# Second expert stage: four experts at a time with 32 places each, instead of two with 64

## The reference, cut to what matters

```
def hier_moe(v, ...):                       # 256 tokens
    grp_prob = softmax(vt @ w_grp + b_grp); p_grp, g_sel = top_k(grp_prob, 1)      # one of 4 groups
    p_in, e_sel = top_k(softmax(expert logits in the group), 2)                    # two of its 8 experts
    combine[t, e] = p_grp * p_in / sum(p_in)                                       # weights, 32 columns
    for e in range(32):
        hdn = silu(vt @ w_gate[e]) * (vt @ w_up[e])        # 1024 -> 512
        y = y + (combine[:, e:e+1] * hdn) @ w_down[e]      # 512 -> 1024
return rms_norm(h + y, g_final)
```

## Time and profile before

| | us |
|---|---|
| median of three runs (range) | 2190.81 (2186.52 to 2191.62) |
| the profiled execution | 2189.51 |
| its span, first to last instruction | 2187.8 |
| of that, second expert stage (from its first product at 1707.87) | 479.9 |
| TensorE busy / DMA mean rate over the span | 95% / 323 GB/s |

### The profile page before, as it was taken

How to read it: one execution, slowest core, us unless ns; L and a number is a source line. 1 busy time by engine, 2 the same in 40 slices (tenths; PEclk the granted TensorE clock), 3 DMA queues, 4 the chain that set the end, 5 groups by cost and what they waited for, 6 DMA issues and landing times. The chain is left out here.

```text
span 2187.8 us, 25313 instructions
## 1 busy us (share of the span) xinstructions
PE 2083.4 (95%) x10244; PEld 1024.6 (47%) x10244; DVE 538.5 (25%) x1147; ACT 366.7 (17%) x628; POOL 98.6 (5%) x185
## 2 busy tenths in 40 slices
PE   6989999989999999999999999899899999999998
PEld 4677676643333333333333333364464444444443
DVE  2356453432121122112111212222343100000001
ACT  2133421210000000000000000213341111111112
POOL 2010052000000000000000000100030000000000
PEclk9999999999999999999999999999999999999999
DMA  9332245559999999999999999834253699999995
GB/s 340 107 126 103 76 182 206 214 234 428 427 428 429 428 429 429 428 429 428 428 429 427 429 429 427 317 116 167 66 207 135 257 426 429 428 428 430 428 428 227
DMA packets 98558, 707.05 MB, mean 323 GB/s; under 512 B 12314, under 2 KB 17932, under 8 KB 61516
## 3 DMA queue, kind: packets, MB, share of 16 engines
q1 hardware_dynamic: 98508, 706.36, 78.6%
HBM read 705.29 MB, written 1.05 MB: 323 GB/s over the span
## 5 line engine op out<-in xcount | busy, mean ns | idle before, releaser
L1647 PE MATMUL ps<-ring,arena 128*64 128x512 f32 x2048 | 449.8, 593 | 24.6 <-DMA ring<-in_moe_w_gu 24.6
L1647 PEld LDWEIGHTS ps<-ring,arena 128*64 128x64 f32 x2048 | 145.6, 137 | 323.3 <-issue 266.5
L2821 PE MATMUL ps<-ring,arena 128*64 128x512 f32 x1024 | 225.4, 593 | 8.5 <-DMA ring<-in_w_up 6.7
L1674 PE MATMUL ps<-ring,arena 128*64 128x512 f32 x1024 | 225.1, 592 | 0.0
L2821 PEld LDWEIGHTS ps<-ring,arena 128*64 128x64 f32 x1024 | 78.8, 137 | 151.8 <-issue 151.8
L1698 ACT ACTIVATE arena<-arena 128x512 f32<-128x512 f32 x32 | 20.1, 630 | 769.8 <-DVE arena L1729 769.8
L1041 PEld LDWEIGHTS ps<-arena 128*128 128x128 f32 x1088 | 128.6, 196 | 41.9 <-issue 38.9
L1674 PEld LDWEIGHTS ps<-ring,arena 128*64 128x64 f32 x1024 | 73.2, 137 | 146.5 <-issue 128.1
L1041 PE MATMUL ps<-arena 128*128 128x128 f32 x1088 | 138.1, 284 | 2.6 <-DVE arena L1033 2.6
L2074 PE MATMUL ps<-ring 128*128 128x512 f32 (+1 forms) x320 | 139.7, 586 | 0.7 <-ACT ring L2453 0.6
L2842 PE MATMUL ps<-ring,arena 128*64 128x512 f32 x512 | 113.4, 595 | 0.0
(11 more groups left out here) (571 smaller groups left out, 1934.5 us busy)
## 6 DMA issues: line engine op xcount, KB each, us to landing
ring<-in_moe_w_gu SPq DMA_DIRECT2D x128, 2048.0 KB, 23.9
ring<-in_moe_w_down SPq DMA_DIRECT2D x64, 2048.0 KB, 21.3
ring<-in_w_down SPq DMA_DIRECT2D x32, 2048.0 KB, 13.3
ring<-in_w_gate SPq DMA_DIRECT2D x32, 2048.0 KB, 14.9
ring<-in_w_up SPq DMA_DIRECT2D x32, 2048.0 KB, 17.2
ring<-in_w_in SPq DMA_DIRECT2D x22, 2048.0 KB, 8.4
ring<-in_ada_w SPq DMA_DIRECT2D x12, 2048.0 KB, 9.6
ring<-in_w_out SPq DMA_DIRECT2D x6, 2048.0 KB, 8.7
```

Of the source, the lines that this page charges most:

```text
L1647: last = M.matmul(ps[halves[j], 4 + which, :], xgT[buf][:, k, CAP * ee:CAP * ee + CAP], w[:, k2, at:at + 512], start=False, stop=(k == KD ...
L1674: last = M.matmul(ps[halves[j], 6, :], yT[:, k % KH, halves[k // KH]], w[:, k % KH, 512 * j:512 * j + 512], start=False, stop=(k == 2 * KH ...
L2821: last = M.matmul(ps[halves[j], 4 + which, :], xgT[:, k, halves[j]], w[j][:, k, :], start=(k == 0), stop=(k == KD - 1))
```

## The change

An expert of the second stage gets CAP2 = 32 places in a pass instead of 64, and four experts (QUAD) are handled at a time, 8 quads instead of 16 pairs. With 29 tokens in the fullest expert there is still one pass.

- The output partitions are split into four strips of 32 (quads). Gate and up products are made for two experts at a time: pair (0, 1), then pair (2, 3), each 8 slices x 2 experts. The down products take all four experts side by side: 2 x 4 x 4 = 32 matmuls of 128 x 32 x 512, after all four down slots have arrived.
- Gather, transposes and scatter come once for a quad instead of once for a pair, with the shapes they had.
- A quad has 12 loads in a ring of 6 slots: gate 0 to 3 in slots 0 to 3, up 0 and 1 in slots 4 and 5, up 2 and 3 in slots 0 and 1, down 0 to 3 in slots 2 to 5. s_done rises once for each pair's gate, once for each pair's up, and by 2 at the end of the down products, which gives back four slots at once. ExpertLoads gets the count of loads and of rounds as parameters; the first experts use it with their old numbers.
- VectorE makes the one-hot of four experts by one comparison of 128 x 256 elements with broadcast operands, and the gated one by one multiplication, instead of 4 + 4 small operations for a pair. A row of numbers 0 to 255 (iota_all) is made once by GpSimd early in the second mixer.
- The tables of places and gates have 36 columns for this stage; GpSimd's later_tables is gone there, two small copies on VectorE and four more steps in pass_count come in.

```diff
-    loads2 = ExpertLoads("experts2", gate_up_down2, 2)
+    loads2 = ExpertLoads("experts2", gate_up_down2, 3 * QUAD, 2, MAXP2)
+    quads = [slice(CAP2 * e, CAP2 * (e + 1)) for e in range(QUAD)]
+    def quad_onehot(onehot, slots, first, ready):
+        V.tensor_tensor(onehot.rearrange("p t (e c) -> p t e c", e=QUAD), rep(rep(first, QUAD), T), bcast(slots, CAP2),
+                        ALU.is_equal).then_inc(ready, 1)
...
             def load(item, base):
-                for s, (src, k, w) in enumerate(self.chunks(item)):
-                    sp.wait_ge(self.s_done, base * self.steps + s // self.per_done + 1)
-                    sp.dma_start(slot(s, k, w), src).then_inc(self.full[s], 16)
+                for c, (src, k, w) in enumerate(self.chunks(item)):
+                    sp.wait_ge(self.s_done, base * self.steps + (c + self.count - SLOTS) // self.per_done + 1)
+                    sp.dma_start(slot(c % SLOTS, k, w), src).then_inc(self.full[c % SLOTS], 16)
...
                         for which in range(2):
-                            w = [loads.arrived(pe, 2 * which + j, i) for j in range(2)]
-                            for k in range(KD):
-                                for j in range(2):
-                                    last = M.matmul(ps[halves[j], 4 + which, :], xgT[:, k, halves[j]], w[j][:, k, :],
-                                                    start=(k == 0), stop=(k == KD - 1))
-                            last.then_inc(s_done, 1)
+                            for pair in ((0, 1), (2, 3)):
+                                w = {e: loads.arrived(pe, QUAD * which + e, i) for e in pair}
+                                for k in range(KD):
+                                    for e in pair:
+                                        last = M.matmul(ps[quads[e], 4 + which, :], xgT[:, k, quads[e]], w[e][:, k, :],
+                                                        start=(k == 0), stop=(k == KD - 1))
+                                last.then_inc(s_done, 1)
...
-                        w = [loads.arrived(pe, 4 + j, i, 4, 1024) for j in range(2)]
+                        w = [loads.arrived(pe, 2 * QUAD + e, i, 4, 1024) for e in range(QUAD)]
                         pe.wait_ge(s_yTt, i + 1)
                         for d in range(2):
                             for k in range(KH):
-                                for j in range(2):
-                                    last = M.matmul(ps[halves[j], (4, 7)[d], :], yT[:, k, halves[j]],
-                                                    w[j][:, k, 512 * d:512 * (d + 1)], start=(k == 0), stop=(k == KH - 1))
+                                for e in range(QUAD):
+                                    last = M.matmul(ps[quads[e], (4, 7)[d], :], yT[:, k, quads[e]],
+                                                    w[e][:, k, 512 * d:512 * (d + 1)], start=(k == 0), stop=(k == KH - 1))
                             if d == 0:
                                 last.then_inc(s_dh, 1)
-                        last.then_inc(s_done, 1)
+                        last.then_inc(s_done, 2)
```

More of the change, by code:

```diff
@@ L21 @@
 CAP = 64
+CAP2 = 32
+QUAD = 4
 class Chain:
@@ L880, in program @@
     iota_row = sb("iota_row", [P, 2, CAP])
+    MAXP2 = T * P // CAP2
+    NI2 = NE + QUAD
+    slot_of2, gate_of2 = ar(13600, T, NI2), ar(13600 + T * NI2, T, NI2)
+    iota_all = masks[:, 0:T, :].rearrange("p a b -> p (a b)")
     passes = sb("passes", [1, 1], I32)
@@ L913, in first_slots, with pass_count @@
         dve.wait_ge(s_slot, 1)
-        vv(V.tensor_scalar(slot_of[:, :, 0:NE], tmp2, -1.0, None, ALU.add))
-    def pass_count(rank_bank):
+        vv(V.tensor_scalar(table[:, :, 0:NE], tmp2, -1.0, None, ALU.add))
+    def pass_count(rank_bank, cap):
         vv(V.tensor_reduce(cmax[:, 0:1], ps[:, rank_bank, 64:96], X_AXIS, ALU.max))
-        vv(V.tensor_scalar(cmax[:, 1:2], cmax[:, 0:1], float(CAP), 1.0, ALU.is_gt, ALU.add))
-        for b in range(2, MAXP):
-            vv(V.scalar_tensor_tensor(cmax[:, 1:2], cmax[:, 0:1], float(b * CAP), cmax[:, 1:2], ALU.is_gt, ALU.add))
+        vv(V.tensor_scalar(cmax[:, 1:2], cmax[:, 0:1], float(cap), 1.0, ALU.is_gt, ALU.add))
+        for b in range(2, T * P // cap):
+            vv(V.scalar_tensor_tensor(cmax[:, 1:2], cmax[:, 0:1], float(b * cap), cmax[:, 1:2], ALU.is_gt, ALU.add))
         vv(V.tensor_copy(passes[0:1, 0:1], cmax[0:1, 1:2]))
@@ L964, in program, with __init__ @@
     class ExpertLoads:
-        def __init__(self, name, chunks, per_done):
-            self.name, self.chunks, self.per_done = name, chunks, per_done
-            self.steps = SLOTS // per_done
+        def __init__(self, name, chunks, count, per_done, most):
+            self.name, self.chunks, self.count, self.per_done, self.most = name, chunks, count, per_done, most
+            self.steps = count // per_done
+            self.rounds = count // SLOTS
             self.full = [sem(f"{name}_slot{s}_full") for s in range(SLOTS)]
@@ L983, in load_rest @@
         def load_rest(self, sp, items):
-            n = sp.value_load(passes[0:1, 0:1], min_val=1, max_val=MAXP)
+            n = sp.value_load(passes[0:1, 0:1], min_val=1, max_val=self.most)
+            for c, (src, k, w) in enumerate(self.chunks(0)):
+                if c >= SLOTS:
+                    sp.wait_ge(self.s_done, (c - SLOTS) // self.per_done + 1)
+                    sp.dma_start(slot(c % SLOTS, k, w), src).then_inc(self.full[c % SLOTS], 16)
             def load(item, base):
-                for s, (src, k, w) in enumerate(self.chunks(item)):
-                    sp.wait_ge(self.s_done, base * self.steps + s // self.per_done + 1)
-                    sp.dma_start(slot(s, k, w), src).then_inc(self.full[s], 16)
+                for c, (src, k, w) in enumerate(self.chunks(item)):
+                    sp.wait_ge(self.s_done, base * self.steps + (c + self.count - SLOTS) // self.per_done + 1)
+                    sp.dma_start(slot(c % SLOTS, k, w), src).then_inc(self.full[c % SLOTS], 16)
             with sp.Fori(0, items - 1) as q:
@@ L999, in load_rest, with arrived @@
             return n
-        def arrived(self, pe, s, i, k=KD, w=512):
-            pe.wait_ge(self.full[s], i * 16 + 16)
-            return slot(s, k, w)
+        def arrived(self, pe, c, i, k=KD, w=512):
+            pe.wait_ge(self.full[c % SLOTS], i * (16 * self.rounds) + 16 * (c // SLOTS + 1))
+            return slot(c % SLOTS, k, w)
     halves = [slice(CAP * j, CAP * (j + 1)) for j in range(2)]
@@ L1555, in _ @@
             V.tensor_tensor(gate_of[:, :, 0:NE], gate_of[:, :, 0:NE], bcast(gs, NE), ALU.mult).then_inc(s_gat1, 1)
-            pass_count(4)
+            pass_count(4, CAP)
             V.memset(y21, 0.0).then_inc(s_y21, 1)
@@ L1976, in program @@
     s_k11 = sem("ranks2_ready")
-    s_gat2 = sem("gates2_normalised")
+    s_iota2 = sem("places_numbered")
     s_slot2 = sem("first_slots2_ready")
@@ L1985, in gate_up_down2 @@
     def gate_up_down2(q):
[L1987 to L1990, removed]
-    loads2 = ExpertLoads("experts2", gate_up_down2, 2)
+        quad = [QUAD * q + e for e in range(QUAD)]
+        return ([(one(w_gt, e).rearrange("(p k) n -> p k n", k=KD), KD, 512) for e in quad]
+                + [(one(w_up, e).rearrange("(p k) n -> p k n", k=KD), KD, 512) for e in quad]
+                + [(one(w_d2, e).rearrange("(p k) n -> p k n", k=4), 4, 1024) for e in quad])
+    loads2 = ExpertLoads("experts2", gate_up_down2, 3 * QUAD, 2, MAXP2)
[3 more added lines that the diff above has]
+                        ALU.is_equal).then_inc(ready, 1)
     FIRST = 6
@@ L2758, in _ @@
             dve.wait_ge(s_e12, 2)
-            vv(V.tensor_tensor(gate_of[:, :, 0:NE], gate_of[:, :, 0:NE], sel, ALU.mult))
-            vv(V.tensor_reduce(gs, gate_of[:, :, 0:NE], X_AXIS, ALU.add))
+            vv(V.tensor_tensor(gate_of2[:, :, 0:NE], gate_of2[:, :, 0:NE], sel, ALU.mult))
+            vv(V.tensor_reduce(gs, gate_of2[:, :, 0:NE], X_AXIS, ALU.add))
             vv(V.tensor_tensor(gs, gs, gsum, ALU.mult))
             vv(V.reciprocal(gs, gs))
-            V.tensor_tensor(gate_of[:, :, 0:NE], gate_of[:, :, 0:NE], bcast(gs, NE), ALU.mult).then_inc(s_gat2, 1)
-            pass_count(4)
+            vv(V.tensor_tensor(gate_of2[:, :, 0:NE], gate_of2[:, :, 0:NE], bcast(gs, NE), ALU.mult))
+            vv(V.tensor_copy(gate_of2[:, :, NE:NI2], gate_of2[:, :, 0:QUAD]))
+            vv(V.tensor_scalar(slot_of2[:, :, NE:NI2], slot_of2[:, :, 0:QUAD], -float(CAP2), None, ALU.add))
+            pass_count(4, CAP2)
             V.memset(y22, 0.0).then_inc(s_y22, 2)
@@ L2771, in program, with expert_quads @@
     s_p13 = sem("final_weight_loaded")
-    def expert_pairs(loads, x_tok):
+    def expert_quads(loads, x_tok):
         KH = 4
-        NP = NE // 2
+        NQ = NE // QUAD
         xgT, sg, y, yT = ar(7168, KD, P), ar(8192, 512), ar(8704, KH, P), ar(9216, KH, P)
@@ L2794, in _ @@
```

(30 more changed lines are left out.)

25 lines of the change are left out of this document (13 added, 12 removed).

## The result

The changed kernel takes 2196.85 us, median of 6 runs (2195.74 to 2199.59); the kernel before, beside it, 2186.73 (2185.03 to 2191.62). The ratio is 1.0036, 95% interval 1.0026 to 1.0047: slower, by about 8 us by the ratio (the two medians are 10.1 apart). The time lies inside the range that was given, the sign is the wrong one.

A forecast was written before the change was run, and what follows sets the result against it. The prediction took the DMA load stream as the bound, by a hair over TensorE. Terms -5.2 - 2.0 - 0.4 = -7.6, + 1.1 + 2.5 = -4.0 us gave 2185.5 us (2186.8 beside the median), 8-in-10 range 2181 to 2201.

The forecast's parts named there:

- The bound: Second expert stage: DMA sets the pace by a hair, 29.3 us a pair, of which TensorE needs 28.8.
- TensorE's work, four strips at once: Down products of four experts run side by side, 7.0 us; some 14 us a quad saved, all beside the stream.
- rival 5: Strips not side by side, +46 us, or more than 32 tokens in an expert, +470 us; chance 0.02.
- The end: Last quad: all other products done before its last down load lands, so the 5.3 us wait shrinks; gain 5.2 us.
- The hole at the start: Stream gap at 1736 to 1740 goes because slots come free sooner; gain 2.0 us.
- Routing: One comparison replaces four small ones on the path to the first gather; 0.4 us saved.
- Four slots at once: Next loads wait for the down products' end, 2.5 us of stream left; 0.15 us x 7 quads, 1.1 us lost.
- far end: Upper bound for the four-slot wait: 2.4 us in each of 7 quads, 16.8 us.
- The clock: TensorE idles 4.0 us ahead of down products; one down in four cold at full price, 2.5 us lost.
- Rival 2: Queue runs dry behind the down products, 2.4 us in each of 7 quads: +9.2, with clock +12, 2200 to 2203; chance 0.17.
- Rival 4: Every down starts cold, 7 x 1.7 us, start-up hidden or nearly: +5.4, 2196; chance 0.08.
- Rivals 1 and 3: 1: start-up and clock cost nothing, 2183, chance 0.23; 3: stream's own holes and charges eat the gain, 2190, chance 0.08.

The follow-up runs named there:

- filler ahead of the down products: Changed kernel plus four extra 128 x 128 x 512 matmuls before the wait for the down loads; 2193.31 us, ratio 1.0017 to the kernel before.
- the filled kernel with 4.0 left: Changed kernel with extra matmuls in every wait of the second expert stage and 3/4 of the down products; 2184.56 us, ratio 0.9978 to the kernel before.
- the filled kernel with 2.2 left: Changed kernel with extra matmuls in every wait of the second expert stage, all down products kept; 2198.40 us, ratio 1.0036 to the kernel before.

## Why the prediction was wrong, point by point

*The bound.* Right: the stream of loads sets the pace, what TensorE saves inside it is worth nothing, the gains lie at its ends and holes.

*TensorE's work, four strips at once.* Right, and with it rival 5 is out: 64 records in 7.07 us where 7.0 was worked out from L267.

*The end.* Right: -5.0 against -5.2. *The hole at the start.* Gone as said, -2.9 against -2.0. *Routing.* Of the stage's 1.2 us earlier start at most 0.2 can be from it: TensorE's wait in the routing ahead of the comparison already ended 1.0 us earlier in this execution.

*Four slots at once: the step that failed.* The prediction named the wait, the 2.5 us left (2.2 to 2.3 measured) and both ends, and chose 0.15 us a quad, on the argument that a start-up of 2.6 us runs beside the last 2.5 us of stream, since "2.5 us is nearer to filled than 1736.75 was". It isn't: at full clock and 2.2 us left the price is 1.8 us on average, at 3.1 still 0.9, and it takes 4.0 to hide it. The term was put at 1.1 us; 15.4 was measured. That alone turns -4 into +10. The rest brings it to the +7.2 between the profiles: clock -0.8 (1.7 for 2.5), hole -0.9, start -0.8, smaller items -0.8, end +0.2.

The trace before held the very case. The prediction took the queue at 1736.75 to be "almost empty" and the median of 12.2 us in the earlier trace rows to be 2.3 us over an empty queue's. By the landing times the up load ahead was there at 1738.92 and the first down load at 1746.70: 2.2 us of stream were left, as in the changed kernel, and 7.78 - 4.89 = 2.9 us were lost. The hole that the change removes and the dips that it brings in are one thing, once before and seven times after. The 2.4 us kept as far end, 16.8 in all, came out near the 15.4, though by a sum that isn't the one of the trace. Of the two loads behind the "empty queue" of the earlier trace rows one was issued with 0.7 us left, and it landed after 7.47 us, where the other took 7.57: there too what was left hid next to nothing.

*The clock.* Sized at 2.5 us for seven down products; one in four of the bound of 1.7 us would be 0.43 and not 0.36 a quad, so 3.0, and the sum -3.5 and not -4.0. Right in kind: the waits ahead of the down products were 3.1 to 4.8 us where 4.0 was worked out, and in five of eight quads of this profile the down products were cold in part, clock 0.71 to 0.83. What it costs: filler ahead of the down products bought about 4 us (ratio 1.0017 against 1.0036 and 1.0040), of which 1.7 is the last quad's down products, which the prediction left out, because nothing is queued behind it. The dips hid the rest: once a start-up is paid, down products that end 1.7 us later cost only a few tenths more.

*The rivals.* Rival 2 was the case, with its mechanism and nearly its price (+9 to +12 us given, +8 by the ratio measured; as times 2200 to 2203 and 2196.85); it had 0.17. What it held against itself, that the DMA engines "were already idle" at 1736.75, was not so. Rival 4's 2196 is the nearest number, by coincidence: not every down product starts cold, start-ups aren't hidden, and with every down product at full clock six quads still lost 1.8 us each. Rivals 1 and 3 are out. The Trainium skill says in "TensorE: Matmul & The Clock Gate", section "HAM oscillation", that where bursts of matmuls alternate with waits for the next weights every burst begins cold. The traces agree in part: the down products behind the 3 to 5 us waits were cold at first in five and six of the eight quads of the two profiles, and warm in the others.

## What to carry to other kernels

In a kernel bound by its stream of weights, count for every place where slots come back how much of the stream is still queued at that moment; here about 4 us were needed (nearly one 2 MB load at 4.9 us; at 4.0 between 0 and 0.9 us was still lost), and "the queue isn't empty" was not enough. Giving back many slots together, after the product that uses them all, is worth less than giving back half of them 5 us earlier, even where that makes the product slower (12.25 us for 7.07). When the trace before has one row that resembles the new situation, work out what was left and what was lost there, and take that price and not that of the comfortable neighbours.

## What the runs showed of the hardware that was not expected

The start-up of a load behind a running one: about 2.5 us lost at 0.25 us left, 1.8 at 2.2, 0.9 at 3.1, none at 4.0 with filled waits. The sixteen completions of a load show where it goes. In every quad with 2.3 us or less left, in all these kernels, the first completion comes 6.5 to 6.9 us after the issue, just as with an empty queue (6.7 for the first load of the earlier trace rows); in the filled kernel with 4.0 left and no loss it comes after 7.8 to 7.9. The last completion is 0.7 to 1.1 us behind the first where 0.25 us was left, and 1.5 to 3.1 us behind it in the filled kernel with 2.2 left: what the stream left over hides is mostly lost again as spread among the engines. Why they spread was not settled; whether another queue would avoid it wasn't tried.

Less TensorE work can take as long: 3/4 of the down products took 7.05 us at a mean clock of 0.76, all of them 7.07 at full clock.

Products for different strips seem to run into each other across the borders of loops; only the times show it. The first three pairs of a stage, with all weights there, took 17.43 us for 96 records, where three times 7.06 is 21.2; two down pairs took 12.25 and not 14.1:

```profile
1706.67 17.43 PE L2845 MATMUL ps<-ring,arena 128*32 128x512 f32 x96 [1.81 <-ACT arena L2881]
```
